# Six matmuls of a weight block, ordered by output bank instead of by pass

## The chip, the cores and the metric

The kernel runs on one core of one Trainium2 chip. The metric is the device time of one execution in microseconds (us). Of the kernel before there are three runs: 2253.70, 2255.86 and 2258.81 us, median 2255.86 us.

## The reference

One decoder layer works on 536 tokens at once: 16 learned meta tokens, 512 prompt tokens and 8 sample tokens. Everything is float32. The heavy part is five matrix products, with two mixers between them:

```
z  = rms_norm(h) @ w_in                 # 2048 -> 4608: conv gates B, C, value; q, k, v
yc = B * conv3(C * xc)                  # short convolution, 1024 channels
ya = attention(rope(q), rope(k), v)     # window 128, 16 heads, 4 kv heads, learned sinks
h  = h + [rms_norm(yc), rms_norm(ya)] @ w_out                       # 2048 -> 2048
h  = h + (silu(n @ w_gate) * (n @ w_up)) @ w_down,  n = rms_norm(h) # 2048 -> 5632 -> 2048
y  = rms_norm(h)
```

The outputs are y for the prompt and the sample tokens, and the new key, value and convolution states.

## The kernel before

**Three passes for one product.** Each weight and each activation is split into a rounded part and the rest of it: `w_hi` and `w_lo`, `a_hi` and `a_lo` (for the third product of the FFN `f_hi` and `f_lo`). A product is the sum of three matmul passes, `w_hi` with `a_hi`, `w_hi` with `a_lo`, and `w_lo` with `a_hi`, all accumulated in the same place in PSUM (the accumulator memory of TensorE). ScalarE makes the rounded part of the weights (line 779) and VectorE the rest (line 1013), from raw weights that SP loads.

**Halves and banks.** The tokens lie along the free dimension and are cut into two halves of 260 columns (262 or 268 where a few columns more are wanted). Each half has its own PSUM bank: `outs[h]` is `pu[slot][:, h, 0:n]`. The pairs of banks are `pu[0]`, `pu[1]` and two pairs in `pa`.

**A unit** (`unit`, lines 383 to 410) makes 128 output columns of a product with 2048 inputs: 16 blocks of 128 by 128 weights, and for each block six matmuls, the three passes times the two halves. It serves the input projection (from its k part on), the output projection (where inputs 0 to 7 and 8 to 15 go to two pairs of banks) and gate and up of the FFN. A unit waits for its weights ahead of blocks 0 and 8, and where `ready` is given for each block's activations (`a_lo_made`) ahead of the block. Its last matmul raises `unit_done`; with `tell` the last matmul of each block raises `act_free`. At some blocks another small job of TensorE is put in (`inserts`): transposes, scores, norms.

**A down tile** (`down_tile`, lines 679 to 693) does the same for `w_down` with four blocks (k = 0 to 3), in the pair of banks `pair[q]`; its last matmul raises `down_done` or `unit_done`.

**The stages.** First x is transposed and normalised, with the v projection beside it (`v_part`, line 439, which the change leaves alone); then the rest of the input projection with attention and convolution woven in; then the output projection; then 11 chunks of the FFN, each with 4 gate and 4 up units and 16 down tiles; the last chunk has the final transposes between its down tiles. VectorE takes both banks of a pair in one instruction after `unit_done` or `down_done` (lines 1270, 1297, 1303, 1318), and raises `free[...]`, for which TensorE waits ahead of the next unit in the pair. TensorE runs its instructions in the order in which they are written; for each matmul there is one weight load in front of it.

Of the kernel before, what the change touches and what calls it, by code (L numbers as in the profile page):

```python
# [201 lines left out]
def build(nc, t):  # L202

    ctx = ExitStack()
    with ctx:
        def sb(c, name, shape, dt=F32):
            return c.enter_context(nc.sbuf_tensor(name, shape, dt))


        w_hi = sb(ctx, "w_hi", [P, 2, UNIT], F32R)  # L210
        w_lo = sb(ctx, "w_lo", [P, 2, UNIT], F32R)
# [37 lines left out]
        with ExitStack() as c2:  # L249
            f_hi = sb(c2, "f_hi", [P, FT, OUT], F32R)  # L250
            f_lo = sb(c2, "f_lo", [P, FT, OUT], F32R)
# [128 lines left out]
        def _(pe):  # L380
            mm = nc.tensor.matmul

            def unit(m, slot, col0, n, inserts=None, ready=None, order=None, tell=False, split=False):

                order = order or range(KT)
                for pos, k in enumerate(order):
                    if inserts and pos in inserts:
                        inserts[pos]()
                    if pos == 0:
                        pe.wait_ge(s.lo_made, 4 * m + 2 * slot + 1)  # L390
                    if pos == 8 or (pos < 8 and k >= 8 and order[pos - 1] < 8):
                        pe.wait_ge(s.lo_made, 4 * m + 2 * slot + 2)
                    if ready:
                        pe.wait_ge(s.a_lo_made, ready + pos)
                    if split:
                        outs = pu[slot] if k < 8 else pa[:, 2 * slot:2 * slot + 2, :]
                        start, stop = k in (0, 8), k in (7, 15)
                        outs = [outs[:, h, 0:n] for h in range(2)]
                    else:
                        outs = [pu[slot][:, h, 0:n] for h in range(2)]  # L400
                        start, stop = pos == 0, pos == KT - 1
                    w = slice(k * P, k * P + P)
                    passes = [(w_hi, a_hi), (w_hi, a_lo), (w_lo, a_hi)]
                    for i, (wt, a) in enumerate(passes):
                        for h in range(2):
                            last = mm(outs[h], wt[:, slot, w], a[:, k, col0 + h * n:col0 + h * n + n],  # L406
                                      start=start and i == 0, stop=stop and i == 2)
                    if tell and pos < KT - 1:
                        last.then_inc(s.act_free, 1)
                last.then_inc(s.unit_done, 1)  # L410
# [83 lines left out]

            pe.wait_ge(s.free0, 1)
            unit(1, 0, 0, W_KV, {4: norm1_sum, 12: turn_v})
            pe.wait_ge(s.free1, 1)
            unit(1, 1, 0, W_KV)

            def scores(g, i):  # L500
# [94 lines left out]
            def mixers(g, last_g=False):  # L595

                for n in range(8):
                    m, slot = 4 * g + (U_P1 + n) // 2, n % 2
                    pe.wait_ge(free[slot], m)
                    if n >= 5:  # L600
                        pe.wait_ge(s.o_copied, 4 * g + n - 4)
                    if last_g and n == 3:
                        pe.wait_ge(s.knat_copied, 2)
                    if last_g and n == 7:
                        pe.wait_ge(s.sexp, 1)
                    if 3 <= n <= 6:
                        scores(g, n - 3)
                    ins = {}
                    if n >= 4:
                        ins[4] = lambda n=n: turn_p(g, n - 4)  # L610
                        ins[12] = lambda n=n, m=m, slot=slot: values(g, n - 4, m, slot)
                    if last_g:
                        if n == 1:
                            ins[8] = knat
                        if n in (2, 3):
                            ins[8] = lambda n=n: kcache(n - 2)
                        if n == 6:
                            ins[2] = lambda m=m, slot=slot: sample_scores(m, slot)
                        if n == 7:
                            ins[2] = sample_turn  # L620
                            ins[8] = sample_values
                            ins[15] = turn_u
                    unit(m, slot, CX0 if n in (2, 3, 5, 6) else N_META, W_CX if n in (2, 3, 5, 6) else W_OUT,
                         ins, tell=last_g and n == 7)
# [54 lines left out]
            def down_tile(c, d, o, q, ks=range(FT)):  # L679

                slot = d % 2
                for k in ks:
                    if d == 0 and o == 0:
                        pe.wait_ge(s.f_lo_made, 4 * c + k + 1)
                    for i, (wt, a) in enumerate([(w_hi, f_hi), (w_hi, f_lo), (w_lo, f_hi)]):
                        for h in range(2):
                            last = mm(pair[q][:, h, 0:W_OUT], wt[:, slot, 512 * k + P * o:512 * k + P * o + P],  # L687
                                      a[:, k, h * W_OUT:h * W_OUT + W_OUT],
                                      start=k == 0 and i == 0, stop=k == FT - 1 and i == 2)
                if o == 3:  # L690
                    last.then_inc(s.unit_done, 1)
                elif ks[-1] == FT - 1:
                    last.then_inc(s.down_done, 1)

            def down_start(c):

                for ks in (range(FT - 1), range(FT - 1, FT)):
                    for o in range(2):
                        if ks[0] == 0:
                            pe.wait_ge(free[o], 8 * c + 30)  # L700
                        down_tile(c, 0, o, o, ks)

            def down(c):
                for d in range(4):
                    pe.wait_ge(s.lo_made, 2 * (12 * c + U_P3 + 8 + d) + 2)
                    if d == 0:
                        down_start(c)
                    for o in range(2 if d == 0 else 0, 4):
                        if o < 2:
                            pe.wait_ge(free[o], 8 * c + d + 30)  # L710
                        elif isinstance(c, int) and c == 0 and d == 0:
                            pass
                        else:
                            pe.wait_ge(free[o], 4 * c + d)
                        down_tile(c, d, o, o)
# [25 lines left out]
            for x in range(KT):  # L741
                d, o = x // 4, x % 4
                if o == 0:
                    pe.wait_ge(s.lo_made, 2 * (12 * c + U_P3 + 8 + d) + 2)
                if x == 0:
                    down_start(c)
                elif x > 1:
                    pe.wait_ge(free[x % 2], 8 * c + 30 + x // 2)
                    down_tile(c, d, o, x % 2)
                if x >= 1:  # L750
                    turn_y(x - 1)
# [823 lines left out]
```

## Time and profile before

| what | value |
|---|---|
| median of three runs | 2255.86 us |
| span of the profiled execution, first to last instruction | 2252.2 us |
| mean granted clock of TensorE | 0.995 |
| TensorE matmul busy / weight load busy | 98% / 97%, 18357 instructions each |
| VectorE, ScalarE, GpSimd busy | 41%, 26%, 16% |
| mean DMA rate | 97 GB/s |

The profile records one execution; its only time is the span, from the first to the last instruction, and 3.7 us lie between it and the median of the runs. Matmuls overlap in their records: one is listed with about 283 ns, although the next starts long before its end. So the pace of TensorE is read from the starts (or from chain pieces, time over count), not from the mean duration of a matmul.

### The profile page before, as it was taken

What the parts mean: (1) busy time and instruction counts of PE and PEld (TensorE: products, weight loads), DVE (VectorE), ACT (ScalarE), POOL (GpSimd) and SP (SyncE); (2) the same over time, 40 slices, a digit from 0 to 9 for tenths busy, and PEclk for the clock granted to TensorE, in tenths of its full rate; (3) what the DMA queues carried; (4) which work ended last, traced back from release to release, by engine and by line L of the source; (5) the groups of instructions that cost most, each with busy time, mean ns of one, the idle gap of its engine ahead of it and who ended that gap; (6) DMA issues with size and microseconds to landing.
All of it is one profiled execution on the core that took longest, in us unless ns stands there. A gap on an engine that the chain in (4) does not pass through costs nothing.

```text
span 2252.2 us, 43181 instructions
## 1 busy us (share of the span) xinstructions
PE 2217.3 (98%) x18357; PEld 2189.5 (97%) x18357; DVE 930.2 (41%) x1099; ACT 591.9 (26%) x780; POOL 362.8 (16%) x310
## 2 busy tenths in 40 slices
PE   7999999999999999999999999999999999999997
PEld 6999999999998999999999999999999999999997
DVE  6743444547446343333433334333343333334335
ACT  4232323243113212212122222222212222221221
POOL 6121212425665000000000000000000000000024
PEclk9999999999999999999999999999999999999998
DMA  8422222322343323233332323223233232332222
GB/s 246 151 69 84 75 84 82 114 81 82 112 114 104 96 94 91 93 94 93 93 93 93 91 90 94 80 96 89 93 93 93 93 93 93 89 91 94 83 91 77
DMA packets 325754, 217.43 MB, mean 97 GB/s; under 512 B 7294, under 2 KB 296678, under 8 KB 325496
## 3 DMA queue, kind: packets, MB, share of 16 engines
q1 hardware_dynamic: 318496, 201.61, 29.9%
q0 software_dynamic: 2048, 8.21, 1.2%
q10 hardware_dynamic: 5160, 6.88, 0.9%
q8 instruction: 39, 0.64, 0.1%
q14 instruction: 11, 0.09, 0.0%
HBM read 207.80 MB, written 10.95 MB: 97 GB/s over the span
## 4 chain that ended last, share of the span: by engine, by line
PE 96%; DVE 2%; POOL 0%; ACT 0%; DMA 0%; issue 0%; ACTq 0%; DVEq 0%; POOLq 0%
PE pu L406 66%; PE pu L687 12%; PE pa L687 10%; PE pa L406 4%; DVE a_lo L1127 1%; PE pa L509 1%; PE pu L529 1%; PE pu L439 1%; PE pa L518 1%; PE pa L738 0%; DVE w_lo L1020 0%; DVE a_hi L1029 0%; DMA cvs<-conv_w 0%; DVE w_lo L1013 0%; DVE a_lo L1032 0%; PE pa L424 0%
## 5 line engine op out<-in xcount | busy, mean ns | idle before, releaser
L406 PE MATMUL pu<-a_hi,w_hi 128*128 128x260 f32 (+2 forms) x4160 | 840.3, 283 | 0.8 <-ACT cvs L824 0.5
L406 PE MATMUL pu<-a_lo,w_hi 128*128 128x260 f32 (+2 forms) x4160 | 839.2, 283 | 0.0
L406 PE MATMUL pu<-a_hi,w_lo 128*128 128x260 f32 (+2 forms) x4160 | 835.9, 282 | 0.0
L406 PEld LDWEIGHTS pu<-a_hi,w_hi 128*128 128x128 f32 x4160 | 640.3, 189 | 13.3 <-issue 11.7
L406 PEld LDWEIGHTS pu<-a_hi,w_lo 128*128 128x128 f32 x4160 | 643.3, 189 | 0.0
L406 PEld LDWEIGHTS pu<-a_lo,w_hi 128*128 128x128 f32 x4160 | 639.3, 188 | 0.0
L1013 DVE TENSOR_TENSOR w_lo<-w_raw,w_hi 128x1024 fp32r<-128x1024 f32 x364 | 464.8, 1317 | 186.8 <-ACT w_hi L779 181.3
L779 ACT ACTIVATE w_hi<-w_raw 128x1024 fp32r<-128x1024 f32 x364 | 364.3, 1048 | 671.6 <-PE pa L687 365.9
L1525 POOL TENSOR_TENSOR xs<-xs,rstd 128x520 f32<-128x520 f32 x44 | 57.9, 1317 | 1389.8 <-ACT xs L973 1389.8
L687 PE MATMUL pu<-f_hi,w_hi 128*128 128x260 f32 x768 | 155.8, 284 | 0.0
L687 PE MATMUL pu<-f_hi,w_lo 128*128 128x260 f32 x768 | 154.7, 283 | 0.0
L687 PE MATMUL pu<-f_lo,w_hi 128*128 128x260 f32 x768 | 154.0, 282 | 0.0
L1297 DVE TENSOR_TENSOR xs<-pu,rstd 128x520 f32<-128x520 f32 x44 | 30.8, 699 | 297.9 <-PE pu L406 297.4
L1303 DVE TENSOR_TENSOR xs<-pu,xs 128x520 f32<-128x520 f32 x44 | 30.8, 700 | 282.5 <-PE pu L406 282.5
L976 ACT ACTIVATE f_hi<-xs 128x520 f32 x44 | 28.1, 640 | 395.0 <-DVE xs L1303 395.0
L687 PE MATMUL pa<-f_hi,w_lo 128*128 128x260 f32 x640 | 129.0, 283 | 0.0
L687 PE MATMUL pa<-f_hi,w_hi 128*128 128x260 f32 x640 | 128.9, 283 | 0.0
L687 PE MATMUL pa<-f_lo,w_hi 128*128 128x260 f32 x640 | 128.2, 281 | 0.0
L1318 DVE TENSOR_TENSOR res<-pa,res 128x520 f32<-128x520 f32 x80 | 56.0, 700 | 173.9 <-PE pa L687 173.9
L687 PEld LDWEIGHTS pu<-f_hi,w_hi 128*128 128x128 f32 x768 | 118.3, 188 | 0.3
L973 ACT ACTIVATE xs<-xs 128x520 f32<-128x520 f32 x44 | 28.1, 638 | 343.7 <-DVE xs L1297 343.7
L687 PEld LDWEIGHTS pu<-f_lo,w_hi 128*128 128x128 f32 x768 | 118.0, 188 | 0.0
(206 smaller groups left out, 1803.0 us busy)
## 6 DMA issues: line engine op xcount, KB each, us to landing
w_raw<-w_gate SPq DMA_DIRECT2D x88, 512.0 KB, 4.6
w_raw<-w_up SPq DMA_DIRECT2D x88, 512.0 KB, 4.4
w_raw<-w_down SPq DMA_DIRECT2D x88, 512.0 KB, 4.0
w_raw<-w_in SPq DMA_DIRECT2D x72, 512.0 KB, 4.9
w_raw<-w_out SPq DMA_DIRECT2D x32, 512.0 KB, 3.9
q_s<-x_t POOLq DMA_DIRECT2D x16, 260.0 KB, 3.7
y_prompt<-y_nat SPq DMA_DIRECT2D x8, 512.0 KB
res<-x_prompt SPq DMA_DIRECT2D x4, 768.0 KB, 7.4
```

Source lines behind the costliest of these rows:

```text
L406: last = mm(outs[h], wt[:, slot, w], a[:, k, col0 + h * n:col0 + h * n + n], start=start and i == 0, stop=stop and i == 2)
L439: last = mm(pu[slot][:, h, 0:W_KV], wt[:, slot, k * P:k * P + P], a[:, k, h * W_KV:h * W_KV + W_KV], start=k == 0 and i == 0, stop=k == KT ...
L509: last = mm(s_ps[:, 2 * pr + hh, :], q_s[r, hh, P * i:P * i + P], k_g[r, P * i:P * i + 256], start=hh == 0, stop=True, skip_group_check=True)
L687: last = mm(pair[q][:, h, 0:W_OUT], wt[:, slot, 512 * k + P * o:512 * k + P * o + P], a[:, k, h * W_OUT:h * W_OUT + W_OUT], start=k == 0 a ...
L779: act.activation(w_hi[:, slot, part], w_raw[:, slot, part], ACT.Copy).then_inc(s.hi_made, 1)
L973: act.activation(t_a, t_c, ACT.Silu).then_inc(s.silu_made, 1)
L976: act.activation(f_hi[:, bass.ds(f, 1), :].rearrange("p a n -> p (a n)"), t_c, ACT.Copy).then_inc(s.f_hi_made, 1)
L1013: dve.tensor_tensor(w_lo[:, slot, part], w_raw[:, slot, part], w_hi[:, slot, part].bitcast(F32), ALU.subtract).then_inc(s.lo_made, 1)
L1297: dve.tensor_tensor(halves(t_c), pu[0][:, :, 0:W_OUT], halves(rstd[:, 0:OUT]), ALU.mult).then_inc(free[0], 1)
L1303: dve.tensor_tensor(halves(t_c), pu[1][:, :, 0:W_OUT], halves(t_a), ALU.mult).then_inc(free[1], 1)
L1318: dve.tensor_tensor(r, pair[q][:, :, 0:W_OUT], r, ALU.add).then_inc(free[q], 1)
L1525: pool.tensor_tensor(t_a, t_a, rstd[:, 0:OUT], ALU.mult).then_inc(s.silu_scaled, 1)
```

## The change

In both helpers the two inner loops change places. Before, each pass went over both halves; now each half goes through its three passes.

```
before: (w_hi,a_hi) h0, h1 | (w_hi,a_lo) h0, h1 | (w_lo,a_hi) h0, h1
after:  h0 (w_hi,a_hi), (w_hi,a_lo), (w_lo,a_hi) | h1 (w_hi,a_hi), (w_hi,a_lo), (w_lo,a_hi)
```

```
@@ unit, line 404
-                    for i, (wt, a) in enumerate(passes):
-                        for h in range(2):
+                    for h in range(2):
+                        for i, (wt, a) in enumerate(passes):
                             last = mm(outs[h], wt[:, slot, w], a[:, k, col0 + h * n:col0 + h * n + n],
                                       start=start and i == 0, stop=stop and i == 2)
@@ down_tile, line 685
-                    for i, (wt, a) in enumerate([(w_hi, f_hi), (w_hi, f_lo), (w_lo, f_hi)]):
-                        for h in range(2):
+                    for h in range(2):
+                        for i, (wt, a) in enumerate([(w_hi, f_hi), (w_hi, f_lo), (w_lo, f_hi)]):
                             last = mm(pair[q][:, h, 0:W_OUT], wt[:, slot, 512 * k + P * o:512 * k + P * o + P],
                                       a[:, k, h * W_OUT:h * W_OUT + W_OUT],
                                       start=k == 0 and i == 0, stop=k == FT - 1 and i == 2)
```

The order of the three passes within a bank stays as it was, and so does the last matmul of a block (third pass, second half).

## Rows read from the trace of the kernel before

**Rows 1.** The page's first part: busy us (share of the span) xinstructions.
```profile
PE 2217.3 (98%) x18357; PEld 2189.5 (97%) x18357; DVE 930.2 (41%) x1099; ACT 591.9 (26%) x780; POOL 362.8 (16%) x310
```

**Rows 2.** The page's chain that ended last, shares of the span.
```profile
PE 96%; DVE 2%; POOL 0%; ACT 0%; DMA 0%; issue 0%; ACTq 0%; DVEq 0%; POOLq 0%
PE pu L406 66%; PE pu L687 12%; PE pa L687 10%; PE pa L406 4%; DVE a_lo L1127 1%; PE pa L509 1%; PE pu L529 1%; PE pu L439 1%; PE pa L518 1%; PE pa L738 0%; DVE w_lo L1020 0%; DVE a_hi L1029 0%; DMA cvs<-conv_w 0%; DVE w_lo L1013 0%; DVE a_lo L1032 0%; PE pa L424 0%
```

**Rows 3.** Waits of TensorE: us in total, times, longest us.
```profile
PE pu L634 <- POOL acc L1371: 5.3, 1, 5.3
PE pa L406 <- DVE a_lo L1127: 1.8, 3, 0.8
```

**Rows 4.** Who waited for TensorE, of all waits.
```profile
DVE xs L1297 <- PE pu L406: 297.4, 43, 8.0
DVE res L1318 <- PE pa L687: 173.9, 80, 2.2
```

**Rows 5.** Groups of matmuls: xcount | busy us, mean ns | idle before, releaser.
```profile
L406 PE MATMUL pu<-a_hi,w_hi 128*128 128x260 f32 (+2 forms) x4160 | 840.3, 283 | 0.8 <-ACT cvs L824 0.5
L406 PE MATMUL pa<-a_lo,w_hi 128*128 128x260 f32 x256 | 51.5, 283 | 0.0
L687 PE MATMUL pu<-f_hi,w_hi 128*128 128x260 f32 x768 | 155.8, 284 | 0.0
L687 PE MATMUL pa<-f_hi,w_lo 128*128 128x260 f32 x640 | 129.0, 283 | 0.0
```

**Rows 6.** The chain in time, one FFN chunk: start us, us, what.
```profile
851.57 91.42 PE pu L406 x768
942.99 5.76 PE pu L687 x48
...
983.23 5.75 PE pa L687 x48
```

**Rows 7.** Timelines of short windows: norm matmuls, each recorded as two in one bank.
```profile
529.58 0.82 PE L634 MATMUL pu<-acc,ones 128*128 128x260 f32 x3
529.80 0.82 PE L634 MATMUL pu<-acc,ones 128*128 128x260 f32 x3
530.02 0.60 PE L634 MATMUL pu<-acc,ones 128*128 128x260 f32 x2
530.46 0.38 PE L634 MATMUL pa<-acc_a,ones 128*128 128x260 f32 x1
```

**Rows 8.** The chain in time: eight transposes; 32 small matmuls into one bank.
```profile
501.37 0.87 PE pa L518 x8
...
505.12 3.58 PE pa L583 x32
```

**Rows 9.** Weight loads of units by form: xcount | busy us, mean ns | idle.
```profile
L406 PEld LDWEIGHTS pu<-a_hi,w_lo 128*128 128x128 f32 x4160 | 643.3, 189 | 0.0
L406 PEld LDWEIGHTS pu<-a_lo,w_hi 128*128 128x128 f32 x4160 | 639.3, 188 | 0.0
```

**Rows 10.** Timeline of TensorE, one block of an FFN unit.
```profile
1000.24 0.40 PE L406 MATMUL pu<-a_hi,w_hi 128*128 128x260 f32 x2
1000.48 0.40 PE L406 MATMUL pu<-a_lo,w_hi 128*128 128x260 f32 x2
1000.72 0.40 PE L406 MATMUL pu<-a_hi,w_lo 128*128 128x260 f32 x2
1000.96 0.39 PE L406 MATMUL pu<-a_hi,w_hi 128*128 128x260 f32 x2
```

**Rows 11.** Timeline of TensorE, a unit of 268 columns: start us, us, instruction.
```profile
67.71 0.41 PE L406 MATMUL pu<-a_lo,w_hi 128*128 128x268 f32 x2
...
71.65 0.41 PE L406 MATMUL pu<-a_hi,w_lo 128*128 128x268 f32 x2
```

**Rows 12.** Clock: whole core; stretches with busy us, PEclk, DMA share, GB/s.
```profile
core 0: 2252.2 us, clock 0.995
760.00:2195.00 1435.00, 1434.83 (x12031) 1434.55 (x12031) 510.53 (x547) 346.85 (x375) 63.82 (x50) 1.00 0.30 91
2195.00:2252.20 57.20, 42.27 (x358) 41.38 (x357) 31.65 (x53) 6.33 (x7) 28.67 (x23) 0.88 0.20 75
```

## The prediction

> **What bounds the kernel now.** I read the busy shares first. TensorE has matmuls in flight for 98% of the span and weight loads for 97%, VectorE for 41% [rows 1]. A busy TensorE need not be one at its peak, so next comes the chain that ended last: 96% of it is TensorE, and the two lines that the change touches, 406 and 687, make up 66 + 4 and 12 + 10 = 92% [rows 2]. Then the waits of TensorE: the only sizeable one near the changed lines is 1.8 us in total for activations at the start of the output projection; the 5.3 us for GpSimd is at the norm [rows 3]. So nothing feeds TensorE late, and the time is number of matmuls times pace. VectorE waits for TensorE, not the other way round: 297.4 us ahead of line 1297 and 173.9 us ahead of line 1318 [rows 4].
>
> The number of matmuls: three passes of 4160 (units in `pu`), 256 (units in `pa`), 768 and 640 (down tiles) [rows 5] (one pass of each shown), that is 3 x 5824 = 17,472 of 18,357, or 2912 blocks of six. The pace: gate and up of a chunk take 91.42 us for 768 matmuls, 119.0 ns each; a pair of down tiles takes 5.75 us for 48, 119.8 ns each [rows 6]. By these two, the changed lines hold about 13,248 x 119.0 + 4224 x 119.8 = 2083 us of the span (a little more where a half has 262 or 268 columns). That is the whole stake: one nanosecond of pace is 17.5 us, and 0.26 ns is 0.2% of the time, about what a measurement of this kernel can tell from no change.
>
> **The change part by part.** *Counts.* No matmul, weight load, wait, DMA or instruction of another engine comes or goes. There are as many weight loads as matmuls, 18,357 of each [rows 1], although four of the six loads of a block bring in what the matmul before already had; so a load is not left out when weights repeat, and none is gained when they repeat less often. Term: 0 us.
>
> *Waits and signals.* The waits for weights, free banks and activations stand ahead of a block, never between its six matmuls, and the last matmul of a block is the same one as before. So `unit_done`, `down_done` and `act_free` are raised at the same place, and no queue is moved past anything; SP, ScalarE and GpSimd issue what they issued. The first bank is complete three matmuls earlier (3 x 119 = 0.36 us), but VectorE reads both banks in one instruction, so nobody can use it; the second bank is begun two matmuls later, 0.24 us, and TensorE had waited for the whole pair. In the `ready` units the block's activations are waited for at its head in both orders. Term: 0 us. If one of these covers were missing, TensorE would show a wait that [rows 3] does not have.
>
> *Banks.* Before, each matmul goes to another bank than its predecessor. Afterwards four of the six steps of a block stay in one bank: 4 x 2912 = 11,648 steps. The trace has no such step at this shape; the nearest rows are the norm matmuls, of the same 260 columns, recorded as two instructions in one bank and then two in the next. They start at 529.58, 529.80, 530.02 and, after one more, in a third bank at 530.46 [rows 7]: staying 0.22 us, changing 0.22 us, and 0.44 us for one of each. No difference within the 10 ns of these figures. But they go at 220 ns apiece, so they could hide a price that 119 ns would show. Ends from further off: 32 matmuls of eight columns, all into one bank, go at 3.58 / 32 = 111.9 ns, eight transposes at 0.87 / 8 = 108.8 ns [rows 8]. If the 3.1 ns between them were the price of staying in a bank, the change would cost 11,648 x 3.1 = +36 us. If, the other way, all that parts 119.0 from those 108.8 ns were the price of changing banks, it would give 11,648 x 10.2 = -119 us. I take 0: it is the answer of the rows that have the same columns, and both far ends have other reasons (other weights and columns).
>
> *Weights and moving data.* Before, a block changes weights twice (to `w_lo`, and to the next block) and repeats them four times; afterwards it changes four times and repeats twice, so 2 x 2912 = 5824 steps turn from repeat to change. The loads with `a_lo,w_hi` are all repeats: 639.3 us for 4160. Of those with `a_hi,w_lo` half are changes: 643.3 us [rows 9]. The 4.0 us over 2080 changes give 1.9 ns at most for a change, and +11 us if all of it came into the pace; the reverse sign would be -11 us. It does not reach the pace now: the three passes of a block start 0.24 us apart whether their loads are repeats or half changes [rows 10]. And the pace follows the columns: at 268 columns 16 pairs take 71.65 - 67.71 = 3.94 us, 123.1 ns a matmul against 119.0 at 260 [rows 11]. So the stream of activations ends last, and a weight load beside it has cover. I take 0.
>
> *Addresses.* What is left is the order in which the halves are read. Gate/up units and down tiles stream the same 260 columns with the same order of passes and yet differ by 119.8 - 119.0 = 0.75 ns [rows 6]; they differ in where their halves and weights lie. After the change each half is still read three times per block from the same addresses, only its neighbours in time are others. I take 0 for it, and 0.75 ns on each of 17,472 matmuls, 13 us, as the bound to both sides.
>
> *Sum.* 0 on a span of 2252.2 us; the median of the three runs shown is 3.7 us above this span, so I forecast the median, 2256 us.
>
> *A rule against this forecast.* In the stretch from 760 to 2195 us, where banks alternate at each matmul, the granted clock is 1.00, that is 2.4 GHz throughout [rows 12]. The Trainium skill, "TensorE: Matmul & The Clock Gate", section "A second HAM failure mode: psum-queue depth-cycling", says that cycling through PSUM banks can leave small gaps in which the clock falls back, by which less cycling should give time. The trace does not bear it out here: there is nothing to give back in that stretch.
>
> **The rivals.**
> *Slower, staying in a bank costs.* The accumulation into the bank that was just written holds the next matmul up, for all 11,648 steps, lines 406 and 687 alike. For it: no row shows the step at full pace, and the two rates of [rows 8] allow 3.1 ns. Against it: [rows 7]. It decides from 4.5 / 11,648 = 0.39 ns a step; at 1 ns the time is 2268 us, at 3.1 ns 2292 us. The same sign, smaller: the 5824 new changes of weights come into the pace at up to 1.9 ns, 2267 us.
> *Faster, the pace settles lower.* Either changing banks has a small price now, or the new neighbours in time suit the two streams better. For it: 119.0 ns is well above the 108.8 of the transposes, and a mere change of addresses makes 0.75 ns. Against it: [rows 7] show no price of a bank change. With 0.75 ns on all matmuls: 2256 - 13 = 2243 us.
> *Faster through the clock.* The mean granted clock of 0.995 [rows 12] leaves 2252.2 x 0.005 = 11 us; of that 57.2 x 0.12 = 7 us is in the last stretch, in which TensorE waits for the final steps. At most 4 us are left: 2252 us, within what counts as no change.
> *The change doesn't reach the engine:* if TensorE's time per matmul is fixed by its 260 columns alone, the order is invisible, which is my forecast by another road, 2256 us.
>
> **How the numbers follow.** No change, 2256 us: 0.54 (with the clock's few us in it). Slower by bank or weight steps or by worse neighbours: 0.26. Faster by a lower pace: 0.20. The likeliest case alone spans 2251 to 2261 us, the 0.2% around it. Cases of both signs hold nearly half of the chance, so the range reaches 13 us down, to 2243, and 14 up, to 2270, where a bank price of 1.2 ns ends; beyond it I leave one in ten on each side.
>
> **What would show it.** Right: gate and up of a chunk again at 91.4 us for 768 matmuls and a pair of down tiles at 5.75 us, the same counts, no new wait of TensorE, granted clock 1.00 in the FFN. The bank rival shows as a longer interval to the second and third matmul of a half only; the weight rival as a longer one at the `w_lo` steps, with longer records of their loads; the address case as steps that differ from block to block with no regard to bank or weight. The prediction is wrong if a chunk's 137.4 us (91.42 + 8 x 5.75) move by more than 0.3 us.

## The result, and the profile after

The changed kernel takes 2263.75 us in the median of five runs (2263.37 to 2264.99), the kernel before 2254.54 us in five; the ratio, from all runs of both, is 1.0038, 95% interval 1.0026 to 1.0051. It is slower by 0.4%, and the interval lies clear of 1. The span of the profiled execution grew from 2252.2 to 2261.4 us, by 9.2 us; the mean granted clock is 0.993 against 0.995.

Counts are the same (18,357 matmuls and weight loads), and TensorE waits for nothing new. The chain in time of the kernel after, one FFN chunk (start us, us, what), answers to [rows 6]:

```profile
855.33 92.05 PE pu L406 x768
947.38 5.77 PE pu L687 x48
953.14 5.73 PE pa L687 x48
...
993.28 6.83 PE pu L406 x57
```

Gate and up of a chunk rose from 91.42 to 92.05 us, 0.63 us or 0.82 ns a matmul. A pair of down tiles *fell* from 5.75 to 5.73 us. A whole chunk went from 137.4 us (91.42 + 5.76 + 7 x 5.75) to 993.28 - 855.33 = 137.95 us, and ten of them make 5.4 us. The first chunk lost 1.5 us: some 0.5 as the others do, the rest through the clock. In its first unit stands the norm, for which TensorE waits 5 us (the first of the waits below), and behind it the granted clock was at its lower level (1.2 GHz) for longer; matmuls start 0.22 us apart there, and 0.12 us at full clock. The first ten us of gate and up behind the norm (us, busy us and instructions of the five engines, PEclk, DMA share, GB/s), before and after:

```profile
722.08:732.08 10.00, 10.00 (x81) 10.00 (x80) 6.73 (x4) 4.52 (x5) 2.38 (x3) 0.94 0.27 106
724.37:734.37 10.00, 10.00 (x72) 10.00 (x72) 6.74 (x4) 4.52 (x5) 2.38 (x3) 0.83 0.28 107
```

Nine matmuls fewer are about 1.1 us. Some 2.3 us were lost ahead of the FFN: 0.5 of them before the first changed matmul, where the change can't be the cause, 0.7 in the input projection, and 1.1 in the output projection, whose units run at the pace of gate and up (48 matmuls took 5.71 us before and 5.75 after). So about 7.7 of the 9.2 us are the pace of the changed matmuls (5.4 + 0.5 + 0.7 + 1.1), and about 1.5 are not.

TensorE's waits in the kernel after (us in total, times, longest), for [rows 3]:

```profile
PE pu L634 <- POOL acc L1371: 5.1, 1, 5.1
PE pa L406 <- DVE a_lo L1127: 1.8, 3, 0.8
```

Weight loads by form after (xcount | busy us, mean ns | idle), for [rows 9]:

```profile
L406 PEld LDWEIGHTS pu<-a_hi,w_lo 128*128 128x128 f32 x4160 | 785.3, 189 | 0.0
L406 PEld LDWEIGHTS pu<-a_lo,w_hi 128*128 128x128 f32 x4160 | 785.0, 189 | 0.1
```

These must not be compared in busy time with [rows 9]: there two loads of a kind stood together and overlapped in their group, now they stand alone. The mean of one is 189 ns, as before. From 760 us on the FFN is at full clock again (us, busy us, PEclk, DMA share, GB/s), for [rows 12]:

```profile
760.00:2195.00 1435.00, 1434.84 (x11982) 1434.63 (x11981) 506.17 (x540) 344.84 (x373) 55.24 (x43) 1.00 0.30 91
```

Single matmuls of an FFN unit after, in the timeline of TensorE (start us, us, instruction), one block and the start of the next, for [rows 10]:

```profile
1004.62 0.28 PE L406 MATMUL pu<-a_hi,w_hi 128*128 128x260 f32 x1
1004.75 0.28 PE L406 MATMUL pu<-a_lo,w_hi 128*128 128x260 f32 x1
1004.87 0.28 PE L406 MATMUL pu<-a_hi,w_lo 128*128 128x260 f32 x1
1004.99 0.28 PE L406 MATMUL pu<-a_hi,w_hi 128*128 128x260 f32 x1
1005.10 0.28 PE L406 MATMUL pu<-a_lo,w_hi 128*128 128x260 f32 x1
1005.22 0.28 PE L406 MATMUL pu<-a_hi,w_lo 128*128 128x260 f32 x1
1005.34 0.28 PE L406 MATMUL pu<-a_hi,w_hi 128*128 128x260 f32 x1
```

The steps are 0.13, 0.12, 0.12, 0.11, 0.12 and 0.12 us. Those that stay in a bank (all but the third and the last) are not the longer ones as a class, though figures of 0.01 us can't tell fractions of that apart.

### The profile page after: what moved, and what is told of

It is laid out like the page before. It is cut to its first block, busy times and chain, and to the rows that moved or that the text cites. A ratio compares the mean times of both kernels' runs of the same rounds, so it can differ in the third digit from the quotient of the medians.

```text
span 2261.4 us, 43181 instructions
## 1 busy us (share of the span) xinstructions
PE 2226.3 (98%) x18357; PEld 2198.2 (97%) x18357; DVE 930.3 (41%) x1099; ACT 592.0 (26%) x780; POOL 362.9 (16%) x310
## 4 chain that ended last, share of the span: by engine, by line
PE 96%; DVE 2%; POOL 0%; DMA 0%; ACT 0%; issue 0%; ACTq 0%; DVEq 0%; POOLq 0%
PE pu L406 66%; PE pu L687 12%; PE pa L687 10%; PE pa L406 4%; DVE a_lo L1127 1%; PE pa L509 1%; PE pu L529 1%; PE pu L439 1%; PE pa L518 1%; PE pa L738 0%; DVE w_lo L1020 0%; DVE a_hi L1029 0%; DMA cvs<-conv_w 0%; DVE w_lo L1013 0%; DVE a_lo L1032 0%; PE pa L424 0%
## 5 line engine op out<-in xcount | busy, mean ns | idle before, releaser
L406 PE MATMUL pu<-a_hi,w_hi 128*128 128x260 f32 (+2 forms) x4160 | 1184.6, 285 | 0.8 <-ACT cvs L824 0.5
L406 PE MATMUL pu<-a_lo,w_hi 128*128 128x260 f32 (+2 forms) x4160 | 1176.3, 283 | 0.0
L406 PE MATMUL pu<-a_hi,w_lo 128*128 128x260 f32 (+2 forms) x4160 | 1176.3, 283 | 0.0
L406 PEld LDWEIGHTS pu<-a_hi,w_hi 128*128 128x128 f32 x4160 | 784.4, 189 | 13.1 <-issue 11.7
L406 PEld LDWEIGHTS pu<-a_hi,w_lo 128*128 128x128 f32 x4160 | 785.3, 189 | 0.0
L406 PEld LDWEIGHTS pu<-a_lo,w_hi 128*128 128x128 f32 x4160 | 785.0, 189 | 0.1
L687 PE MATMUL pu<-f_hi,w_hi 128*128 128x260 f32 x768 | 218.0, 284 | 0.0
L687 PE MATMUL pu<-f_hi,w_lo 128*128 128x260 f32 x768 | 216.2, 282 | 0.0
L687 PE MATMUL pu<-f_lo,w_hi 128*128 128x260 f32 x768 | 216.2, 282 | 0.0
L687 PEld LDWEIGHTS pu<-f_hi,w_lo 128*128 128x128 f32 x768 | 144.3, 188 | 0.0
```

## The experiments

**Banks, weights or activations (four kernels).** The change moves three things at once: the bank that a matmul writes, the weights it loads and the half that it reads. Each kernel here takes the six matmuls of a block from a list, in `unit` and `down_tile` alike, and combines the orders of before and after:

```
-                    for i, (wt, a) in enumerate(passes):
-                        for h in range(2):
-                            last = mm(outs[h], ..., start=start and i == 0, stop=stop and i == 2)
+                    for i, (wx, ax, h, b) in enumerate(ORDER6):
+                        wt, a = (w_hi, w_lo)[wx], (a_hi, a_lo)[ax]
+                        last = mm(outs[b], ..., start=start and FIRST[i], stop=stop and LAST[i])

                    weights               activations (part, half)    banks
before              hi hi hi hi lo lo     h0 h1 l0 l1 h0 h1           0 1 0 1 0 1
after               hi hi lo hi hi lo     h0 l0 h0 h1 l1 h1           0 0 0 1 1 1
e1_banks_only       before                before                      after
e2_operands_only    after                 after                       before
e3_weights_only     after                 before                      before
e4_moving_only      before                after                       before
```

> The six matmuls read weights and activations in the order of before, but the first three of a block write to the first bank and the last three to the second, so four of six steps stay in a bank as in the changed kernel (this mixes the two token halves in the sums: only its time is meant). Bank theory (a step that stays in a bank costs): all of the change's loss comes back, span 2252.2 + 9 = 2261 us, gate and up of a chunk at 92.05 us as in the changed kernel. Read-order theory (the loss comes from the order in which weights and activations are read): as before, span 2252 us, gate and up 91.42 us.

> The reverse: weights and activations are read in the order of the changed kernel, but the banks alternate at each matmul as before (the halves are mixed in the sums). Bank theory: span 2252 us and gate and up 91.42 us, as before. Read-order theory: span 2261 us, gate and up 92.05 us, a pair of down tiles 5.73 us, as in the changed kernel.

> Only the order of the weights is that of the changed kernel (w_hi, w_hi, w_lo, twice); activations and banks go as before, so wrong pairs are multiplied. A price of changing weights: four changes per block as in the changed kernel, span 2261 us, gate and up 92.05 us, the steps next to w_lo longer. If the order of the activations decides: span 2252 us, gate and up 91.42 us.

> Only the order of the activations is that of the changed kernel (each half read three times in a row); weights (four w_hi, two w_lo) and banks go as before, so wrong pairs are multiplied. If the order of the activations decides: span 2261 us, gate and up 92.05 us. If changes of weights cost: span 2252 us, gate and up 91.42 us.

| kernel | median us (runs) | ratio to before, 95% interval | span |
|---|---|---|---|
| e1_banks_only | 2254.60 (10) | 0.9998, 0.9988 to 1.0007 | 2256.8 |
| e2_operands_only | 2263.87 (5) | 1.0038, 1.0024 to 1.0052 | 2263.2 |
| e3_weights_only | 2254.42 (10) | 0.9998, 0.9988 to 1.0007 | 2252.2 |
| e4_moving_only | 2263.72 (5) | 1.0035, 1.0021 to 1.0049 | 2262.7 |

The same chunk in the chain of each, gate and up and one pair of down tiles; first e1_banks_only:

```profile
850.53 5.75 PE pa L690 x48
856.28 91.42 PE pu L409 x768
```

e2_operands_only:

```profile
851.47 5.73 PE pa L690 x48
857.20 92.06 PE pu L409 x768
```

e3_weights_only:

```profile
845.94 5.75 PE pa L690 x48
851.69 91.42 PE pu L409 x768
```

e4_moving_only:

```profile
850.92 5.73 PE pa L690 x48
856.66 92.05 PE pu L409 x768
```

The order of the activations alone carries the whole effect, both the loss in the units and the small gain in the down tiles, to 0.01 us. Bank and weight order carry none: 11,648 steps that stay in a bank, and 5824 more changes of weights, cost nothing. (The span of e1_banks_only is 4.6 us above that of before, all of it ahead of this chunk, 856.28 against 851.57 us. There the granted clock was lower: 0.57 against 1.00 from 52 to 60 us, 0.66 against 0.83 from 508 to 518 us. Its median shows no such thing.)

**Is it the place of the halves, or the pattern of jumps (four kernels).** The halves follow one another in memory, so in the order of before a half is followed by its neighbour, in the order after mostly by the same half of the other part. Against that "jump" theory stands the address theory: only where the halves lie counts. Two layouts, each in both orders. In f the halves come to lie 320 columns apart, and so at the same place within 256 bytes:

```
-            f_hi = sb(c2, "f_hi", [P, FT, OUT], F32R)
+            f_hi = sb(c2, "f_hi", [P, FT, 2 * 320], F32R)
...
-                                      a[:, k, h * W_OUT:h * W_OUT + W_OUT],
+                                      a[:, k, 320 * h:320 * h + W_OUT],
```

and in the FFN the halves of a lie 264 columns apart in rows of 528, in the same tile:

```
+        n_hi, n_lo = [x[:, :, :].rearrange("p k n -> p (k n)")[:, 0:2 * KT * 264].rearrange(
+            "p (k h n) -> p k h n", k=KT, h=2)[:, :, :, 0:W_OUT] for x in (a_hi, a_lo)]
...
-                            last = mm(outs[h], wt[:, slot, w], a[:, k, col0 + h * n:col0 + h * n + n],
+                            last = mm(outs[h], wt[:, slot, w], a[:, k, h, :] if ffn else a[:, k, col0 + h * n:col0 + h * n + n],
```

> The order of before, but in f_hi and f_lo (the activations of the down tiles) every half starts 320 columns after the last one, so that all halves start at the same place within 256 bytes; same columns, same work (the sample output moves to another place, and GpSimd waits for an earlier store ahead of one load, both off the path). Address theory (where the halves that follow each other lie decides the pace): a pair of down tiles leaves 5.75 us, either way, and agrees with the next run, which has the other order. Theory of the jump (what counts is whether a half is followed by its neighbour or by itself, wherever they lie): 5.75 us or worse here, and 5.73 us in the next. Gate and up stay at 91.42 us. Span 2252 us plus or minus 176 tiles x the change of a tile.

> The changed kernel with the layout of the run before: halves of f 320 columns apart. Address theory: a pair of down tiles takes the same as in that run, to 0.01 us, since with equal starts the order of the halves can't matter. Theory of the jump: 5.73 us against 5.75 us there. Gate and up 92.05 us. Span that of the run before plus 7 to 10 us from the units.

> The order of before, but in the FFN the halves of a_hi and a_lo lie 264 columns apart (260 used) and the rows 528, in place of 260 and 536: other starts, same columns, same work. Address theory: gate and up of a chunk leave 91.42 us, either way, by something like the 0.75 ns x 768 = 0.6 us that parts the layouts seen so far. Theory of the jump: 91.42 us, as before. Down tiles 5.75 us a pair.

> The changed kernel with the layout of the run before (halves of a in the FFN 264 columns apart). Theory of the jump: gate and up 0.63 us per chunk above the run before, as 92.05 is above 91.42, since the order is the same. Address theory: the difference between the two orders is another one, smaller or of the other sign. Down tiles 5.73 us a pair.

The medians are 2256.70, 2265.46, 2265.72 and 2265.14 us; the ratios to before 1.0003 (0.9993 to 1.0013), 1.0041 (1.0027 to 1.0055), 1.0044 (1.0027 to 1.0060) and 1.0042 (1.0028 to 1.0056). The chain of e5_f320_pass:

```profile
845.98 5.76 PE pa L687 x48
851.74 91.44 PE pu L406 x768
```

e6_f320_bank:

```profile
849.91 5.76 PE pa L687 x48
855.67 92.05 PE pu L406 x768
```

e7_a264_pass:

```profile
847.66 5.75 PE pa L689 x48
853.40 92.38 PE pu L408 x768
```

e8_a264_bank:

```profile
849.95 5.73 PE pa L689 x48
855.68 92.17 PE pu L408 x768
```

With equal starts the down tiles take 5.76 us in either order: the 0.02 us between the orders are gone. That e5 would leave 5.75 us clearly was a miss: it moved by 0.01. With the halves of a 264 columns apart both orders are slower than 91.42 us, and the order after is now the quicker one, 92.17 against 92.38 us. So the sign of the change's effect depends on the layout, and the jump theory, by which the order after should cost 0.63 us again, falls.

The traces show it from nearer, block by block. This is the time from the start of a block's six matmuls to the start of the next block's, in ns, in kernels with the order of before (worked out from the starts in the traces, mean over the chunks behind the first that are whole in the trace):

| kernel, stage | blocks in turn | activations of the next block lie |
|---|---|---|
| before, units, blocks 8 to 15 | 715.8, 707.5, 715.0, 711.7, 725.0, 702.5, 725.0, 710.8 | 2144 bytes on |
| e7_a264_pass, units, blocks 8 to 15 | 714.2, 715.0, 738.4, 719.0, 714.3, 715.0, 738.4, 718.9 | 2112 bytes on |
| before, down tiles, blocks 0 to 3 | 720.3, 722.0, 712.9, 719.1 | 2080 bytes on |
| e5_f320_pass, down tiles, blocks 0 to 3 | 720.5, 720.0, 720.0, 720.0 | 2560 bytes on |

Within a stage every block has the same six matmuls with the same order of weights and banks, and its weights lie a whole number of 256 bytes on from the last block's. Yet the blocks differ, by the same amounts from unit to unit and from tile to tile (with a standard deviation of about 0.5 ns in the units, 1 to 3 ns in the down tiles). Of the four rows they are alike only in the last, where all halves start at the same place within 256 bytes. That is the sign which the prediction had named for the address case: steps that differ from block to block with no regard to bank or weight.

**A third order, the best of both, and absolute addresses.** e9_mixed makes the change in `down_tile` only. e10_back_and_forth reads the halves in the order 0 1, 1 0, 0 1; e11_f320_moved is e5 with 160 bytes ahead of f (by the build's addresses every half then starts at a multiple of 256 bytes, where in e5 it starts 96 bytes past one); e12_one_column reads a single column over and over in the down tiles:

```
e10:  -                        for h in range(2):
      +                        for h in ((1, 0) if i == 1 else (0, 1)):
e11:  +            sb(c2, "lead", [P, 40])
e12:  -                                      a[:, k, h * W_OUT:h * W_OUT + W_OUT],
      +                                      a[:, k, h * W_OUT:h * W_OUT + 1].to_broadcast([P, W_OUT]),
```

> Units pass by pass as before, only the down tiles bank by bank: from each the order that was quicker in its own layout. Address theory: gate and up 91.42 us (before), a pair of down tiles 5.73 us (changed kernel), span 2252.2 - 176 tiles x 0.006 = 2251 us, a gain too small to be told from none in the times. If the order of one stage acts on the other: another value in one of the two rows.

> A third order of the halves: first, second in pass one; second, first in pass two; first, second in pass three; weights as before, the steps in one bank are two of six. Address theory: a pace of its own for each layout, not on the line between the two known orders: gate and up between about 91 and 92.4 us, the down pair between 5.70 and 5.77. If only the number of repeats of a half counts (none before, four of six in the changed kernel): 2 of 4 of the way, gate and up 91.74 us, down pair 5.74 us.

> The first layout run (order of before, halves of f 320 columns apart) with all of f moved by 160 bytes, so that every half starts at a multiple of 256 bytes. If where a half lies in absolute terms decides the pace: a down pair leaves 5.76 us, better for the even start. If only the steps from one half to the next decide: 5.76 us as there. Gate and up 91.42 us, span 2253 us if nothing moves.

> The down tiles read one column of f 260 times over in place of 260 columns (so their products are others), all else as before. If reading the activations from different addresses makes the pace: a down pair falls from 5.75 us, at most to 48 x 109 = 5.2 us (the transposes' pace), span down to 2252 - 88 x 0.5 = 2206 us. If 260 columns through the array, or the weight loads, make it: 5.75 us and 2252 us as before.

| kernel | median us (runs) | ratio to before, 95% interval | span |
|---|---|---|---|
| e9_mixed | 2254.62 (11) | 0.9998, 0.9989 to 1.0007 | 2251.7 |
| e10_back_and_forth | 2270.81 (4) | 1.0069, 1.0054 to 1.0085 | 2266.1 |
| e11_f320_moved | 2261.67 (8) | 1.0028, 1.0018 to 1.0039 | 2258.5 |
| e12_one_column | 2223.20 (1) | one run, before 2255.97 | 2221.2 |

The chain of e9_mixed:

```profile
846.04 5.73 PE pa L687 x48
851.77 91.44 PE pu L406 x768
```

e10_back_and_forth:

```profile
850.74 5.76 PE pa L687 x48
856.50 92.25 PE pu L406 x768
```

e11_f320_moved:

```profile
847.02 5.81 PE pa L688 x48
852.83 91.44 PE pu L407 x768
```

e12_one_column:

```profile
845.57 5.36 PE pa L687 x48
850.93 91.42 PE pu L406 x768
```

e9 keeps the better row of each kernel, as forecast; its gain, half a microsecond of span, can't be told from none. e10 is slower than both known orders in both stages (92.25 us, and 5.76, there by 0.01 us only), so the pace does not lie on a line between them, and a count of repeats, which would give 91.74, does not explain it. e11 shows that it counts where the halves lie, not only how they lie to one another: against e5 only f moved (and `g_fin` behind it, which no down tile reads), and a pair went from 5.76 to 5.81 us, 88 pairs 4.4 of the 5.0 us of span; each of the four blocks takes 726.7 ns, where those of e5 take 720. Since the weights stayed, e11 does not tell whether the place itself counts or the distance to the weights. My guess that the even start would be the better one was wrong. e12 shows what reading from many addresses costs: with one column in place of 260 addresses a pair takes 5.36 us, 111.7 ns a matmul in place of 119.8, and 88 pairs x 0.39 = 34 us is the order of the 31.0 us that the span lost. Its four blocks are alike, 670 ns each, although the halves start where they do in the kernel before. Its clock stayed at 0.994.

## Why the prediction was right or wrong

**What bounds the kernel: right.** The time moved mainly by the pace of the changed lines (7.7 of 9.2 us), and TensorE stayed the chain.

**Counts, waits and signals, 0 us: right.** Same counts, same waits, nobody used the earlier bank. One figure was off, and nothing hangs on it: the first bank is complete with the third matmul of six in place of the fifth, two earlier (0.24 us) and not three.

**Banks, 0 us: right, and now shown** by e1 and e2. The far ends from [rows 8], +36 and -119 us, had nothing in them; [rows 7], with the same columns, were the rows to follow.

**Weights, 0 us: right, shown** by e3 and e4.

**Addresses, "I take 0 for it": the step that failed.** Its bound was 0.75 ns a matmul, taken from two layouts in [rows 6]; measured were +0.82 ns in the units (0.63 us over 768), more than the bound, and about -0.2 ns in the down tiles (eight pieces of 48 in a chunk, 45.99 us before and 45.90 after). The term is some +7.7 us in place of 0. What misled me was the sentence that each half is still read three times from the same addresses, as if the cost belonged to a half. It belongs to the sequence and the place together: e7 and e8, with the same halves in two orders, differ with the other sign. By the sign that the prediction set itself it was wrong: a chunk was not to move by more than 0.3 us, and moved by 0.54. The likeliest case, no change, did not come true, and of the slower cases it was "worse neighbours", named in half a line, and not the bank price that I had put first. The result, 2263.75 us, still lies within the range of 2243 to 2270. That is in part luck: the upper end was set by a bank price of 1.2 ns that does not exist. The address bound, 2256 + 13 us, would have held the result too, since on the mean of all 17,472 matmuls only some 0.4 ns came out.

**The clock: right in the FFN, not ahead of it.** In the stretch from 760 us on it was 1.00 in both kernels. The prediction counted only what the clock could give back; in the profiled execution it took about 1 us more at the start of the FFN (0.83 against 0.94 above). Such stretches come with the activations in the order of before as well (0.57 and 0.66 in e1), so this is not shown to be the work of the change. The Trainium skill, "TensorE: Matmul & The Clock Gate", section "A second HAM failure mode: psum-queue depth-cycling", tells of a kernel in which cycling through PSUM banks left small gaps and the clock swung between its levels, by which less cycling should have given time; the traces show nothing to be had there. With four of six bank changes gone the clock from 760 us on is 1.00 as before and the kernel is slower; e2, which alternates banks, runs as the kernel after does.

**What stays open.** Why the place and the sequence of addresses make the pace is not shown. e12 says that reading 260 addresses costs 8 ns over reading one, but not whether the reads collide with the weight load beside them or with something else; no kernel here removed the weight loads, and those that moved activations against the weights (e5, e7, e11) moved them against every fixed boundary too. So which layout is quick has to be measured.

## What to carry to other kernels

Where TensorE runs without gaps, an edit that changes no count and no wait can still move the time by some tenths of a per cent, through the order and the place in which the moving operand is read; give that term a size, not a zero. Alternating PSUM banks or staying in one, and repeating weights or changing them, made no difference at this shape. To find out which of several things that move together is the cause, cross them in kernels that do the same work in time, and read the pace from chain pieces at full clock, which repeat here to 0.01 or 0.02 us in 91, where the runs spread by 0.2%; read the granted clock of the other stretches before giving their loss to the change.

## What the runs showed of the hardware

The pace of a matmul of 260 columns ranged from 119.0 ns (91.42 us for 768) to 121.0 ns (5.81 us for 48) by the place and order of its activations alone, and fell to 111.7 ns when it read one column. Within one unit of the kernel before, blocks of six took from 702 to 725 ns, in the same series in each unit. A start of every half at a multiple of 256 bytes gave the slowest of all. If all 17,472 matmuls could run at 111.7 ns, that would save 17,472 x 7.3 ns or more, some 128 us, an estimate from e12 and the units' pace that no real layout here came near.
